# Retention moved behind the first key panel, and modulation sums moved to other stages, in a two-layer block kernel

## The reference, cut to what matters

```python
mod = silu(c) @ w_ada + b_ada                  # 1024 x 6144: twelve panels of 512 columns
sh1, sc1, gt1, sh2, sc2, gt2 = split(mod, 6)   # panels 4,5 = gt1; 6,7 = sh2; 8,9 = sc2; 10,11 = gt2
q = mla_queries(cq, ...); k, v = mla_keys(ckv, ...); kc, vc = mla_keys(ckv_ctx, ...)   # w_uq, w_ukv
o_mla = latent_attention(q, k, v, kc, vc)      # 8 heads, 256 queries, 256 + 256 keys, dim 96
o_ret = retention_bidir(rq, rk, rv, rg, ...)   # per-head groupnorm, times silu(rg)
x = x + gt1 * (concat([o_mla, o_ret]) @ w_out)
x = x + gt2 * conv_ffn(modulate(rmsnorm(x, g_norm2), sh2, sc2), w_up, conv_w, conv_b, w_down)
# second layer: HGRN2 scan (f = sigmoid, log, cumsum, exp), sliding-window attention, cross attention, FFN
```

## Time and profile before

| | us |
|---|---|
| median of 3 runs | 881.71 |
| profiled execution | 880.92 |
| its span | 878.8 |
| TensorE busy | 835.8 |
| VectorE busy | 590.9 |
| ScalarE busy | 464.5 |
| GpSimd busy | 18.3 |

### The profile page before, as it was taken

The page is one execution under the profiler, slowest core; times in us unless marked ns, Lnnn a source line. Parts: engine busy times, 40 slices in busy tenths (PEclk is TensorE's granted clock), DMA queues, the critical chain, the costliest instruction groups (busy, mean ns, idle before and its releaser), DMA issues. The chain is left out here.

```text
span 878.8 us, 12682 instructions
## 1 busy us (share of the span) xinstructions
PE 835.8 (95%) x4868; PEld 719.0 (82%) x4868; DVE 590.9 (67%) x922; ACT 464.5 (53%) x750; POOL 18.3 (2%) x24
## 2 busy tenths in 40 slices
PE   4789999799999999999999999999999999999997
PEld 3588888667789999998789977787987788888785
DVE  4955976979777777786557567667556655555454
ACT  5736365244546666665436666365554655445342
POOL 0001000000000000000000000010000000000000
PEclk9989999989999999999999999999999999999999
DMA  9942683446576666655465754235615456665551
GB/s 338 348 156 73 191 262 111 127 138 214 170 228 199 178 184 184 179 186 193 158 202 187 226 161 153 72 95 171 191 48 168 144 180 182 190 192 186 174 167 48
DMA packets 103507, 152.85 MB, mean 174 GB/s; under 512 B 6506, under 2 KB 55702, under 8 KB 103448
## 3 DMA queue, kind: packets, MB, share of 16 engines
q1 hardware_dynamic: 101160, 145.48, 52.8%
q10 hardware_dynamic: 2288, 6.57, 2.0%
HBM read 150.97 MB, written 1.05 MB: 173 GB/s over the span
## 5 line engine op out<-in xcount | busy, mean ns | idle before, releaser
L1979 DVE TENSOR_TENSOR w_lo<-raw,w_hi 128x1024 fp32r<-128x1024 f32 (+1 forms) x244 | 293.9, 1213 | 167.8 <-ACT w_hi L1449 167.1
L1449 ACT ACTIVATE w_hi<-raw 128x1024 fp32r<-128x1024 f32 (+1 forms) x244 | 253.8, 1050 | 200.4 <-PE bank L723 140.2
L721 PE MATMUL bank<-w_hi,hT_hi 128*128 128x512 f32 (+2 forms) x400 | 156.8, 392 | 5.4 <-DVE hT_lo L2038 2.8
L723 PE MATMUL bank<-w_hi,hT_lo 128*128 128x512 f32 (+2 forms) x400 | 153.9, 385 | 0.0
L722 PE MATMUL bank<-w_lo,hT_hi 128*128 128x512 f32 (+2 forms) x400 | 153.6, 384 | 0.0
L825 PE MATMUL bank<-hT_hi,w_hi 128*128 128x256 f32 x512 | 145.1, 283 | 2.3 <-DVE w_lo L1979 2.3
L826 PE MATMUL bank<-hT_lo,w_hi 128*128 128x256 f32 x512 | 144.9, 283 | 0.0
L827 PE MATMUL bank<-hT_hi,w_lo 128*128 128x256 f32 x512 | 144.9, 283 | 0.0
L825 PEld LDWEIGHTS bank<-hT_hi,w_hi 128*128 128x128 f32 x512 | 98.3, 192 | 2.5 <-DVE w_lo L1979 2.5
L826 PEld LDWEIGHTS bank<-hT_lo,w_hi 128*128 128x128 f32 x512 | 98.3, 192 | 0.0
L827 PEld LDWEIGHTS bank<-hT_hi,w_lo 128*128 128x128 f32 x512 | 98.3, 192 | 0.0
(11 more groups left out here) (338 smaller groups left out, 1189.3 us busy)
## 6 DMA issues: line engine op xcount, KB each, us to landing
raw<-w_up_dram SPq DMA_DIRECT2D x132, 256.0 KB, 3.3
raw<-w_ada_dram SPq DMA_DIRECT2D x48, 512.0 KB, 4.7
raw<-w_down_dram SPq DMA_DIRECT2D x44, 512.0 KB, 4.3
raw<-w_in_dram SPq DMA_DIRECT2D x40, 512.0 KB, 4.5
raw<-w_gate_dram SPq DMA_DIRECT2D x44, 256.0 KB, 2.8
raw<-w_out_dram SPq DMA_DIRECT2D x16, 512.0 KB, 3.4
raw<-wk_x_dram SPq DMA_DIRECT2D x8, 512.0 KB, 4.6
raw<-wv_x_dram SPq DMA_DIRECT2D x8, 512.0 KB, 3.3
```

The costliest lines, as they stand in the source:

```text
L721: pe.matmul(o, xh, yh, start=first, stop=False, skip_group_check=skip)
L723: return pe.matmul(o, xl, yh, start=False, stop=last, skip_group_check=skip)
L1449: act.activation(unit_view(w_hi[n % NSPLIT], u), unit_view(raw[u % NRAW], u), ACT.Copy).then_inc(w_hi_ready, 1)
L1979: dve.tensor_tensor(unit_view(w_lo[n % NSPLIT], u), unit_view(raw[u % NRAW], u), unit_view(w_hi[n % NSPLIT], u).bitcast(F32), ALU.subtract ...
```

## The change

- Sums: the order is now 4, 5, 6, 7, 8, 9, 10, 11. Fourteen units (6, 7, 8, half of 9) stand behind ukv1's first unit instead of 22; the eight units of panels 10 and 11 stand behind units of down0 and down1. There VectorE does one of a sum unit's two instructions ahead of the down unit's `w_lo` and one behind it.
- The spreads of panels 6, 7, 8 leave the attention and stand between the units of w_out0; the spreads 10 and 11 stand behind the eighth unit of down0 and down1, and ScalarE's copies of these gates move into `square_gated`.
- TensorE's order is ukv0, q turns, retention, key turns of panel 0, ukv1, key turns of panel 1. VectorE does the rope keys and the context's values of panel 0 ahead of the retention's statistics, the key copies of panel 0 beside the power, and the second panel's behind the gating. `kT` becomes two tiles, one over rqT and rkT and one over decay, and ScalarE no longer waits for `ret_out_ready`. Eight keep-busy transposes stand ahead of the first score.
- VectorE copies rkT, ScalarE rqT, the latter now ahead of the gate's Silu.
- In the attention VectorE feeds four sum units in five rounds.
- At down0's end ScalarE and VectorE feed one unit more per row tile between the squares and the gated rows.
- `g_post` is fetched by SP behind the last unit of qa; VectorE splits qh's last unit ahead of `bmid` and kva's first ahead of `logf`.

The hunks below stand in this order: planning, memory, TensorE (retention, first attention, w_out0, down), SP, ScalarE (`square_gated`), VectorE (`feed_units`, ahead of the attention, in it, `gated`, behind the scans).

```diff
-SUMMED = (4, 5, 10, 11, 6, 7, 8, 9)
-SUMMED_EARLY = (4, 5, 10, 11)
-SUMS_BESIDE = {**{(name, n): 1 for name in ("rv", "rq") for n in range(4)}, ("ukv1", 0): 22,
-               ("wout1", 0): 1, ("wout1", 1): 1}
+SUMMED = (4, 5, 6, 7, 8, 9, 10, 11)
+GATES = (4, 5, 10, 11)
+SUM_AFTER = {8: (4, 5), 10: (6, 7)}
+SUMS_BESIDE = {**{(name, n): 1 for name in ("rv", "rq") for n in range(4)}, ("ukv1", 0): 14,
+               ("wout1", 0): 1, ("wout1", 1): 1,
+               **{(f"down{p}", n): 1 for p, n in ((0, 0), (0, 2), (0, 4), (0, 6), (0, 8), (0, 10), (1, 4), (1, 6))}}
-BUSY = {"ffnpre": 14, "gu0": 8}
+BUSY = {"score": 8, "ffnpre": 14, "gu0": 8}
...
-        at[0] = after_rows
-        kT = sb("kT", [P, MLA_H, 2 * TOK])
+        at[0] = decay_at
+        kT1 = sb("kT1", [P, MLA_H // 2, 2 * TOK])
+        at[0] = h_at
+        kT0 = sb("kT0", [P, MLA_H // 2, 2 * TOK])
+        kT = (kT0, kT1)
...
+            keys(0)
+            four = [next_small() for _ in range(4)]
...
+            retention(four[0:2])
+            turn_keys(0, four[2:4] * 2)
+            keys(1)
+            turn_keys(1, four[2:4] + four[0:2])
-            sum_spread(10)
-            sum_spread(11)
...
+                        if i == start:
+                            keep_busy(o[:, 0:P], BUSY["score"])
...
-                    if n in (5, 9, 13):
-                        sum_spread(MLA_PANELS[n // 4 - 1], 2)
...
+            next(wout0)
+            sum_spread(6)
+            next(wout0)
+            sum_spread(7)
+            next(wout0)
+            sum_spread(8)
             run(wout0)
...
+                for p in range(2):
+                    steps = rows_steps(f"{down}{p}", act_hi, act_lo, None if p else before)
+                    for _ in range(8):
+                        next(steps)
+                    sum_spread(10 + p)
+                    run(steps)
...
+                if u == last_unit["qa"]:
+                    sp.wait_ge(res_ready, RES["down"])
+                    for n, g in enumerate(("g_mix_post_2", "g_x_post_2", "g_ffn_post_2")):
+                        sp.dma_start(g_post[:, n, :], a[g].partition_broadcast(P)).then_inc(in_post, 16)
...
+                    if extra:
+                        feed_units(last_unit[f"{panel_name}{p}"] + 1)
+                        copy_gate(10 + p)
                     feed(f"{panel_name}{p}", p)
                     for t in range(T):
+                        if extra and not p:
+                            feed_one()
...
+                    if units[u][0].startswith("down") and u + 1 < len(units) and summed[u + 1]:
+                        if units[u + 1][1]:
+                            dve.wait_ge(unit_ready, u)
+                        accumulate(u + 1, range(units[u + 1][1], units[u + 1][1] + 1))
...
+            values(0)
+            more_sums(2)
...
-            more_sums(1)
+            keys_turned(0)
...
+            more_sums(1)
+            values(1)
+            keys_turned(1)
...
-                        feed_units(min(base_unit + n + 1, first_unit["wout0"]))
+                        feed_units(min(base_unit + 3 + 4 * (n + 1) // 5, first_unit["wout0"]))
...
+                        if name == "down":
+                            emptied(dve, ("spread", 10 + p))
+                        elif name == "wout" and p == 0:
+                            for q in (6, 7, 8)[2 * t:2 * t + 2]:
+                                spread(q)
...
+                            if p == 0:
+                                feed_units(fed[0] + 1)
...
+            feed_units(last_unit["qh"] + 1)
             dve.tensor_tensor(by_chunk(bmid), by_chunk(cum), at_position(CH // 2 - 1), ALU.subtract).then_inc(cum_ready, 1)
+            feed_units(first_unit["kva"] + 1)
             dve.tensor_tensor(by_chunk(logf), at_position(CH - 1), by_chunk(cum), ALU.subtract).then_inc(cum_ready, 1)
```

More of the change, by code:

```diff
@@ L992, in _, with keys @@
             sum_spread(5)
[L993 to L1011, removed]
+            def keys(p):
                 name = f"ukv{p}"
@@ L1020, in _, with turn_keys @@
                            (ckvT_hi[:, :, TOK:], ckvT_lo[:, :, TOK:]))
[L1021 to L1031, removed]
+            def turn_keys(p, banks):
                 for t in range(2 * T):
                     use = ("kT", p, t)
-                    o = claim(use, next_small())
-                    emptied(pe, (name, t))
+                    o = claim(use, banks[t])
+                    emptied(pe, (f"ukv{p}", t))
                     pe.wait_ge(kpe_ready, 2 * T)
@@ L1155, in before @@
                         pe.wait_ge(act_lo_ready, NFF * gen + k // 2 + 1)
-                rows_panel(f"{down}0", act_hi, act_lo, before)
-                rows_panel(f"{down}1", act_hi, act_lo)
+                for p in range(2):
+                    steps = rows_steps(f"{down}{p}", act_hi, act_lo, None if p else before)
[3 more added lines that the diff above has]
+                    run(steps)
             def gated_rows(pre):
@@ L1617, in _ @@
             for t in range(T):
+                use = ("rT", "rq", t)
+                ready(act, use)
+                free(act.activation(rqT[:, :, t * P:(t + 1) * P],
+                                    ps(use)[:, :].rearrange("p (h t) -> p h t", h=RH), ACT.Copy), use)
+            for t in range(T):
                 use = ("rg", t)
@@ L1620, in _ @@
                 free(act.activation(sgate[:, t, :], ps(use)[:, :], ACT.Silu), use)
-            for what, dst in (("rk", rkT), ("rq", rqT)):
-                for t in range(T):
-                    use = ("rT", what, t)
-                    ready(act, use)
-                    free(act.activation(dst[:, :, t * P:(t + 1) * P],
-                                        ps(use)[:, :].rearrange("p (h t) -> p h t", h=RH), ACT.Copy), use)
             for p in range(2):
@@ L1642, in _ @@
                 feed_units(last_unit["ukv1"] + 1)
+                for t in range(T):
+                    use = (f"ukv{p}", t)
+                    ready(act, use)
+                    v = ps(use)[:, :].rearrange("p (h d) -> p h d", h=4)
+                    if p:
+                        ready(act, ("kT", 0, t))
+                    act.activation(V[:, t, 4 * p:4 * p + 4, :], v[:, :, NOPE:], ACT.Copy)
+                    free(act.activation(k_row[:, t, :, 0:NOPE], v[:, :, 0:NOPE], ACT.Copy), use)
                 if p == 0:
@@ L1954, in accumulate @@
                         ins = dve.scalar_tensor_tensor(acc, w, csilu[:, 0, k:k + 1], acc, ALU.mult, ALU.add)
-                    elif chunk in SUMMED_EARLY:
+                    elif chunk in GATES:
+                        for p in SUM_AFTER.get(chunk, ()):
+                            ready(dve, ("spread", p))
                         dve.wait_ge(in_gate, 32)
@@ L1959, in accumulate @@
                     else:
-                        if chunk in (6, 8):
-                            for p in SUMMED_EARLY[chunk - 6:chunk - 4]:
-                                ready(dve, ("spread", p))
+                        for p in SUM_AFTER.get(chunk, ()):
+                            ready(dve, ("spread", p))
                         ins = dve.tensor_scalar(acc, w, csilu[:, 0, 0:1], None, ALU.mult)
@@ L2223, in _ @@
             feed_units(min(reach(last_unit["rg"] + 1), last_unit["ukv1"] + 1))
+            for t in range(T):
+                use = ("rT", "rk", t)
+                ready(dve, use)
+                free(dve.tensor_copy(rkT[:, :, t * P:(t + 1) * P], ps(use)[:, :].rearrange("p (h t) -> p h t", h=RH)), use)
             for d in range(2):
@@ L2413, in prenorm @@
                 scale_rows(name, [res[:, 0, :]], [row[:, 0, :]])
-            for p in SUMMED_EARLY:
+            for p in (4, 5):
                 emptied(dve, ("spread", p))
```

111 lines of the change are left out of this document (62 added, 49 removed).

## The result

After the change the kernel takes 868.13 us (median of 4 runs, 867.02 to 870.14), before it 880.80 us in the same comparison; the ratio is 0.9855 with a 95% interval of 0.9831 to 0.9879.

What follows compares the result with a forecast made beforehand. TensorE was taken to bound the kernel, with waits on VectorE and ScalarE between solid stretches. Terms -6.5 - 0.5 + 1.0 - 2.3 = -8.3 gave 872.6 us profiled, 873.4 beside the median; range 869.5 to 878.

Steps and rivals of the forecast that it cites:

- Step 1: Before the retention: rkT copies on VectorE, rqT ahead of the gate's Silu, remove a TensorE wait; -0.26 us.
- Step 2: Up to the first score: retention behind the first key panel, its norm overlapped with other work; -6.5 us, Step 1 included.
- Step 3: First attention with fewer sums and no spreads: -3.1 us; +2.6 for spreads moved into w_out0; net -0.5.
- Spread 8: Attention: taking panel 8's spread out gains nothing there, since round 14 waits for ScalarE rounding a w_out unit.
- the rounds: Attention: eleven instead of fourteen sum units bring rounds from 2.28 towards TensorE's 2.19; at most some 0.7 us.
- Step 4: Down projection: sums and spreads of panels 10 and 11 move there, extra feeds remove a 1.23 gap; net +1.0 us.
- Step 5: Behind the scans: g_post on SP and w_lo ahead of bmid and logf close the 2.32 gap; -2.3 us.
- A: Up to the first score: only part of Step 2 arrives, TensorE idles and the clock falls; 876.9 us, chance 0.17.
- B: Attention: the spreads were hidden where they stood, so +1.1 instead of -0.5; 875.0 us, chance 0.10.
- C: Down projection: the eight sums land on the path at 1.54 each, +12.3; slower, 885.7 us, chance 0.03.
- D: SP's queue: g_post ahead of qh's weights makes TensorE wait up to 4.4 us; 877.8 us, chance 0.05.
- E: Better: VectorE not late before the first score, rounds at 2.19, Step 4's 0.3 not paid; 871.2 us, chance 0.10.

Runs made afterwards that it cites:

- kernel 4: Kernel after the change, with the retention ahead of the first key panel again on TensorE and VectorE, sums still out: 874.82 us, ratio 0.9922.
- kernel 6: Kernel after, with the eight sum units of panels 10 and 11, their spreads and gate copies ahead of the attention, old sum cadence: 881.84 us, ratio 1.0004.
- kernel 1: Kernel after, with a sum unit in every round of the first attention from round 0: 869.40 us, ratio 0.9860.
- kernel 2: Kernel after, with the spreads of panels 6, 7 and 8 back in the attention: 869.74 us, ratio 0.9885.
- kernel 12: Kernel after, without the extra w_hi and w_lo feeds between the squares and gated rows of down0: 868.93 us, ratio 0.9853.
- kernel 10: Kernel after, with g_post's transfers issued by ScalarE again and the feeds at the scans kept: 868.53 us, ratio 0.9849.
- kernel 11: Kernel after, without the two feeds between the scans, bmid and logf, g_post still on SP: 869.84 us, ratio 0.9879.
- kernel 7: Kernel after, with the third sum unit ahead of the retention statistics instead of behind the gating: 872.05 us, ratio 0.9895.
- kernel 8: Kernel after, without the eight filler transposes ahead of the first score: 868.21 us, ratio 0.9860.
- 3: Kernel after, with VectorE's sum ahead of the division of the finished output group in the first attention: 866.57 us, ratio 0.9835.
- 5: Kernel after, with both the retention ahead of the first key panel and VectorE's sum ahead of the division: 867.31 us, ratio 0.9842.
- kernel 9: Kernel after, with the third sum unit ahead of the retention statistics and the sum ahead of the division: 865.44 us, ratio 0.9813.

## Why the prediction was wrong

**Step 1** (-0.26): the wait is gone, and from the turns of rq to the retention states it is 2.97 us instead of 3.38. None of the runs undid it alone.

**Step 2 (-6.5, measured -7.96)** failed in size by 1.46 and in what it was ascribed to. Its times, moved by the 1.36 of the start: retention over at 167.4, measured 166.59. The 0.85 was there when the first key panel started (151.69): a spread pair holds TensorE for 1.3 us and not for the 1.88 of its rows (from 150.37), and what stands ahead of it came 0.3 sooner. Behind that, sixteen turns take 1.75 (157.69 to 159.44) and not 2.1, and the panel and the retention as much longer (13.15, not 12.8). GpSimd's power took 1.64, not 2.11. That gives 0.85 and about 0.5 of the 1.46. VectorE is late next as forecast: its last copy ends at 178.50, the first score starts at 178.82. But the order of the retention, on which the step's text rests, is worth 0.54 (kernel 4). What failed first is the reading that the k_row copies come late because the norm stands ahead of them: in kernel 4 it still does, and the wait is 0.38 and not 2.45. Within the step stood the words "one sum unit, 1.54", where the kernel before does eight units in the stretch and this one three; the gaps of 2.45 and 2.60 stood behind such units. The gain hung on the five that left, with the two spreads, and I had booked the sums' move in step 4, as a cost. The total did not suffer by this; the explanation did. Kernel 6 shows it: the change without that move is worth nothing that can be measured (1.5 us by its stages).

**Step 3 (-3.1, measured -4.80)** failed by two terms. Round 1 (0.87 in the trace, 1.19 by kernel 1): with no sum in round 0 the second maximum comes at once. I had given the start 0.2 in all, and 0.22 came already ahead of the first turn (2.90 us from the first score, before 3.12). Spread 8 (0.84): "round 14 waits for ScalarE" was wrong; the round came 1.30 behind the one ahead, and kernel 2 gives the spread back. The other terms held: the rounds about 0.5 (forecast 0.7), spread 6 0.90 (forecast 0.87), spread 7 hidden with the gap grown to 1.45 (forecast 1.4), the last gap gone (1.40, forecast 1.35), +2.54 in w_out (forecast +2.6).

**Step 4 (+1.0, measured +0.58)** was right in mechanism. The spreads cost 0.86 each and not 0.94, the sums 0.4 together where I charged 0.3, and the extra feeds take off 1.49 (kernel 12), where I had 1.23. The stage moved 253 GB/s (383 to 447 us), near the 270 I had put. VectorE's waiting for ScalarE, "half the time" in the step, is 14.5 of 38 us in rows 7.

**Step 5 (-2.3, measured -2.58)**: right, but only one of its two parts does it. The feeds alone close the gap (kernel 10); g_post's move alone leaves 1.27 of it (kernel 11).

**The rivals.** A did not come: from 170 to 190 us the clock is 1.00. B is refuted by kernel 2 for two of the three spreads. Its price was off as well: it leaves out the 0.7 of the rounds, which stands in step 3's sum; with it B is 874.3. E counts that 0.7 a second time. C is refuted by kernel 6 with 0.4 us for eight sums. D: with g_post on SP's queue the slowest landing of a weight there went from 8.3 to 9.9 us, with g_post issued by ScalarE again (kernel 10) it is 8.0, and TensorE waited for none; kernel 10 is not faster. The rule of the Trainium skill ("DMA: Bandwidth & Descriptors", section "Queues, rings and completion order"), that a ring is consumed in order, agrees with weights that land later behind g_post; no engine that splits weights waits for a transfer there. E had the right direction by the wrong terms: VectorE was late as forecast, and the 0.3 of step 4 was paid; what came beside the forecast are round 1, spread 8 and the faster stretch to the first score. I gave it 0.10. The best bounds of all steps together are 4.0 us better than the forecast (1.2, 1.9, 0.6 and 0.3), 869.4, and there I closed the range, as if no bound could be passed; step 2 passed its own, -7.7, by 0.26. By the stages, -12.2 from the base of 881.71 is 869.5, the very edge of the range. The 1.4 below it are the base, since the median of before was 881.71 in the runs that I had and 880.80 in those beside the result, 0.9 less, and 0.5 by which the medians differ more than the stages.

**What stays open.** Behind the 1.45 gap at round 10 the clock fell in the profiles of kernels 4, 7 and 11 and not in those of after, 6, 8, 10 and 12, which have the same gap, nor in that of 1 with 1.09. Kernel 11 has the same instructions as after up to there; two of its six runs took 873.4 and 874.9, the other four 869.6 to 870.0. So it is not fixed by the program. What decides was not found. The Trainium skill ("TensorE: Matmul & The Clock Gate", section "Part 1: The HAM clock gate (the "warmup" mystery)") says that the monitor behind the clock runs free of the program, so that one kernel can meet it at different phases, and says so of the clock's rise at a kernel's start; the mixed runs agree, and no run here shows the phase. Of the gap itself the runs say this: of the 12 runs of the kernels without the gap (3, 5, 9) none lies more than 2.2 us above the fastest of its kernel. Kernel 2, with two smaller gaps, had runs of 873.5 and 876.9 beside four of 868.8 to 870.3. The two have no profile, but their mean granted clocks are 0.986 and 0.983 beside 0.991 to 0.994, so the clock was low for longer in them; where, isn't on record. The slowest run of after, 870.14, has 0.986 beside 0.992 to 0.997 too: one profile without the fall does not clear a kernel of it.

## What to carry to other kernels

When work is moved off an engine, book the gain where it left and the cost where it lands, and undo each part alone before one is named as the cause: here the re-ordering in the title was worth 0.5 us, and most of the first stage's 8 came with eight sums, and their two spreads, moved to a stretch where VectorE idled. On an in-order engine look at every wait of 1.5 us or more and ask what independent work stands right behind it: two such swaps (kernel 9) gave 2.7 us more. Take the cost of a small TensorE instruction from the distance between starts and not from its busy time.

## Not expected of the hardware

- A gap of 1.45 us in a run of small matmuls (128x64 and 128x128) was followed in some executions by 7 to 14 us at a granted clock of 0.50 (6.8 in kernel 11, 10.2 in kernel 4, 13.6 in kernel 7), and in others, of the same instructions, by none. The price was 3 to 6.5 us, more than twice the gap. A change upstream that shortened its own stage by 1.21 (kernel 7) made the kernel 3.9 us slower in this way.
- TensorE idling 1.94 of 5 us (kernel 8, 175 to 180) did not lower the clock.
- The power on GpSimd over 128x8 took 2.11 us before, where VectorE does a sum beside it, and 1.64 after, where it does two copies, and 1.64 in kernel 4, where it idles. That the sum is the cause was not tested.
